# State-space angles in turns, later input tables, and other places for ada slabs, their sums and the last Toeplitz issues

## The chip, the cores and the metric

The kernel runs on 1 core of one Trainium2 chip. The metric is the device time of one execution in microseconds (us). Before the change the median of three runs is 2386.61 us (2385.92 to 2390.32).

The engines: PE is TensorE (matrix products; it also loads its weights, PEld), DVE is VectorE, ACT is ScalarE, POOL is GpSimd. SP issues most DMAs; ACT issues the others out of its own instruction queue. Each engine works its queue in order and meets the others at semaphores.

## The reference, cut to what matters

Two transformer-like blocks follow each other on 512 tokens of width 1024. The change lies in block one:

```python
z = rms_norm(x, g) @ w_in            # q k v f gf u gs qm gm gl
y_fox = forgetting_attention(q, k, v, log_f) * silu(gf)
y_s5  = gelu(s5_ssm(u, ...))         # 48 groups, 64 complex states each
y_s5  = y_s5 * sigmoid(y_s5 @ w_glu + b_glu) * silu(gs)
mk, mv = split(rms_norm(mem, g) @ w_mem_kv)
y_mem = memory_attention(qm, mk, mv) * silu(gm)
x = x + merge(y_fox, y_s5, y_mem) @ w_out
# block two needs   ada = silu(c) @ w_ada + b_ada   (two layers, 6144 columns each)
```

The state-space layer uses powers of `a = exp(lam * step)`: magnitudes, and cosines and sines of `k * Im(lam) * step` for k = 0 to 8, and of multiples of the eighth power's angle for 64 chunks of 8 tokens.

## The kernel before, in words

Weights come as slabs of 256 columns (1 MB for 1024 rows) through a ring of three slots, loaded by SP in the order of `plan_slabs` (L239). A slab's load waits until the slab three places earlier has been used up. Most slabs are then split by POOL, half by half, into a rounded high part (L234) and a rest (L236), and PE multiplies high by high, low by high and high by low (L589 in streams, L461 in tile stages). The slabs of w_glu and w_mem_kv are not split.

*ada.* Its 48 slabs are no PE work: ACT scales the slab (`ada_scale`), DVE sums it over its rows of tiles (`ada_add`, L376, 3.7 us), PE adds over partitions in a product of one column (`ada_sum`, L389) and DVE adds the bias (`ada_take`, L399). Only two sums may be under way: `ada_add` of slab n waits for `ada_sum` of n-2, and `ada_sum` of n for `ada_take` of n-1. `plan_slabs` puts an ada slab behind another slab. `tiles_stage` (L403) has ACT and DVE work on it at the tile of that slab less `ada_lead`, and has PE and DVE do sum and take three tiles later; what falls past the last tile is handed to the next stage.

*The state-space stage* (`s5_stages`, L1198) runs while PE works through a stream of 37 tiles (u, gs, q, k, f, v; 24 products each). The stream is cut at written positions: `turn_at`, `pad_at`, `out_at` say after how many products PE turns to the state space. There are six parts of 8 groups. For each part: DVE makes the drive table Bk (`drive_table`), an angle table (`angle_table`), and the output table W (`out_table`); PE turns Bk (L1441), makes the Toeplitz blocks from W (L1450), the drive (L1462), and the output y (L1475, L1476). ACT copies the Toeplitz blocks into `pad` and issues eight DMAs to lay them into TT (L1517). ACT also empties the stream's two PSUM banks, at written positions of its own queue (`stream.take`). A tile's product can't begin before the tile two earlier is taken.

*The angles.* `reduce_angle` (L1183) takes an angle in radians, finds the whole turns by adding and subtracting 1.5 * 2^23, subtracts them in three parts of 2 pi, and clamps: six DVE instructions, each waiting for the one before. It is called for the 48 step angles, for their nine multiples (432 columns, `tE`), and once a part (512 columns). ACT then takes Sin of the angle and of its half. For `tE` the half angle is one more DVE instruction (L1610). *The input tables* B1, B2 are made in two goes: part 0 alone (128 columns), and, behind the first drive and angle table, the other 40 groups (640 columns), ahead of the first W (L1686 to L1689).

*Behind the stream* come the six glu tiles (three w_glu slabs), in which ada 0 and ada 1 are worked on; then gf and qm, in whose stage the memory rows are normalised and turned; the forgetting attention; the memory keys and values (eight tiles, three ada slabs); gm with memory attention; then merge. `spread_forget` is a turn of SP bound to the slab behind glu_z2: it writes the summed gates to memory, waits for them, and reads them back spread out, 1.5 MB.

Of the kernel before, what the change touches and what calls it, by code (L numbers as in the profile page):

```python
# [10 lines left out]
ALU = mybir.AluOpType  # L11
ACT = mybir.ActivationFunctionType
# [20 lines left out]
PARTS = G5 // G6  # L33
# [10 lines left out]
TWO_PI = 2.0 * math.pi  # L44
PI_1 = 6.28125
PI_2 = float(np.float32(TWO_PI - PI_1))
PI_3 = float(TWO_PI - PI_1 - float(np.float32(TWO_PI - PI_1)))
PI_TOP = 3.1415925
LN2_1 = 0.693359375
LN2_2 = math.log(2.0) - LN2_1  # L50
ROUND = 1.5 * 2.0 ** 23
# [187 lines left out]
def plan_slabs(K, T):  # L239
# [60 lines left out]
    for i in range(3):  # L300
        add(f"glu_z{i}", T["w_glu"][0], (0, 768), 0, 768, False, part=i)
        if i < 2:
            ada(0)
# [99 lines left out]
def tiles_stage(K, tiles, banks, act=None, dve=None, act_on=None, after=None, entry=None, arriving=None, tensor_entry=None, act_lead=4,  # L403
                also=None, ada_bank=7, late=None, entry_at=None, waits=None, ada_lead=2):

# [26 lines left out]
    if ada and dve is None:  # L432
        raise ValueError("ada's slabs belong to stages in which VectorE takes the tiles")
    rest = [s for n in range(N - 3, N) for s in ada.get(n, [])]
    if late is not None:
# [10 lines left out]
    with K.stage(entry, arriving[2] if arriving else tensor_entry) as block:  # L446

        @block.tensor
        def _(pe):
# [25 lines left out]
            for n, t in enumerate(tiles):  # L475
                if n < first:
                    continue
                if entry_at is not None and n == entry_at[0]:
                    for sem, value in entry_at[1].values():
                        pe.wait_ge(sem, value)  # L480
                if n >= bufs:

                    pe.wait_ge(taken.sem, t0 + n - bufs + 1)
                if n in after:
                    pe.wait_ge(taken.sem, t0 + after[n] + 1)
                for j in range(len(t)):
                    if waits is not None and (n, j) in waits:
                        pe.wait_ge(*waits[(n, j)])
                    ins = product(n, j)
                ins.then_inc(made.sem, 1)  # L490
                for s in ada.get(n - 3, []):
                    ada_sum(K, pe, s, ada_bank)
# [28 lines left out]
        if dve is not None:  # L521
            @block.vector
            def _(e):
                for n in range(N):
# [5 lines left out]

                    for s in ada.get(n - 3, []):
                        ada_take(K, e, s, ada_bank)
# [649 lines left out]

def reduce_angle(K, e, x, t, done=None):  # L1183

# [4 lines left out]
    for part in (PI_1, PI_2, PI_3):  # L1189
        step(v.scalar_tensor_tensor(x, t, -part, x, ALU.mult, ALU.add))  # L1190
    x = v.tensor_scalar(x, x, -PI_TOP, PI_TOP, ALU.max, ALU.min)
    if done is None:
        step(x)
    else:
        x.then_inc(done.sem, 1)


def s5_stages(K, T, arriving):  # L1198
# [214 lines left out]
    with K.stage(before, arriving[2]) as block:  # L1413
# [67 lines left out]
        def _(e):  # L1481
            e.dma_start(K.scratch_x.rearrange("(t p) n -> p t n", p=P), K.xT[:, :, :]).then_inc(xa.sem, 16)
            stream.take(e, 144)
            e.wait_ge(ready.sem, 3)
            nc.scalar.activation(tB[:, :, :], tE[:, :, :], ACT.Sin).then_inc(acted.sem, 1)
            nc.scalar.activation(tC[:, :, :], tA[:, :, :], ACT.Sin).then_inc(acted.sem, 1)
            stream.take(e, START - 24)
# [9 lines left out]
            def make_sines(n):  # L1497
                e.wait_ge(angles.sem, n + 1)
                nc.scalar.activation(sinj[n % 2], cosj[n % 2][:, :, :], ACT.Sin).then_inc(sines.sem, 1)
                nc.scalar.activation(half[:, :, :], cosj[n % 2][:, :, :], ACT.Sin, scale=0.5).then_inc(sines.sem, 1)  # L1500
                e.wait_ge(sines.sem, 2 * n + 2)
# [4 lines left out]
            def lay_toeplitz(n):  # L1506
# [9 lines left out]
                for r in range(CH):  # L1516
                    e.dma_start(TT5[r * H5:(r + 1) * H5, :, :], pad[:, :, r * H5:r * H5 + P]).then_inc(laid.sem, 16)  # L1517

            def swapped(src, signal):
# [53 lines left out]
        def _(e):  # L1573
# [20 lines left out]
            step(v.tensor_tensor(angle8[:, :], lam[:, 1, :], lam[:, 2, :], ALU.mult))  # L1594
            reduce_angle(K, e, angle8[:, :], one(tA))
            kk = K.counts[:, 0:CH + 1].unsqueeze(2).broadcast_to([P, CH + 1, G5])
# [10 lines left out]
            step(v.tensor_tensor(tE[:, :, :], angle8[:, :].unsqueeze(1).broadcast_to([P, CH + 1, G5]), kk, ALU.mult))  # L1607
            reduce_angle(K, e, tE[:, :, :], tA[:, :, :])
            step(v.tensor_copy(angle8[:, :], tE[:, CH, :]))
            v.tensor_scalar(tA[:, :, :], tE[:, :, :], 0.5, None, ALU.mult).then_inc(ready.sem, 1)  # L1610
            e.wait_ge(acted.sem, 2)
# [52 lines left out]
            def angle_table(n):  # L1664
                x = cosj[n % 2][:, :, :]
                step(v.tensor_tensor(x, angle8[:, part(n)].unsqueeze(2).broadcast_to(shape2),
                                     K.counts[:, 0:NC5].unsqueeze(1).broadcast_to(shape2), ALU.mult))
                reduce_angle(K, e, x, tmp[:, :, :], angles)

# [14 lines left out]
            drive_table(0)  # L1684
            angle_table(0)
            input_table(slice(G6, G5)).then_inc(ready.sem, 1)  # L1686
            e.wait_ge(ready.sem, 4)
            v.memset(pad[:, :, 0:112], 0.0).then_inc(K.sig("pad_cleared").sem, 1)
            out_table(0)  # L1689
            for n in range(PARTS):  # L1690
# [4 lines left out]
                if n + 1 < PARTS:  # L1695
                    angle_table(n + 1)
                e.wait_ge(drive_swapped.sem, n + 1)
                e.wait_ge(cosines.sem, n + 1)
# [372 lines left out]
def mem_stages(K, T):  # L2071
# [39 lines left out]
    last = []  # L2111
    tiles_stage(K, tiles, 1, dve=dve, also=also, ada_bank=6, late=last)
    tanh.total += 6
# [865 lines left out]
```

## Time and profile before

| what | value |
|---|---|
| median of three runs | 2386.61 us |
| the profiled execution's own time | 2388.54 us |
| its span | 2386.8 us |
| PE busy | 2284.7 us, 96% |
| DVE busy | 1514.0 us, 63% |
| ACT busy | 619.7 us, 26% |
| POOL busy | 1278.5 us, 54% |
| mean granted TensorE clock | 0.981 of full |

Busy is the time in which an engine had an instruction in work. Idle time of an engine counts only where it holds up the chain that ends last. The granted clock is a share of TensorE's full 2.4 GHz; its other level, 1.2 GHz, is 0.5. In rows, "[3.39 <-DVE Bk L1657]" means that the engine was idle for 3.39 us before this instruction and that the instruction at L1657, on DVE, ended it.

### The profile page before, as it was taken

What the parts mean: (1) busy time and instruction counts of PE and PEld (TensorE: products, weight loads), DVE (VectorE), ACT (ScalarE), POOL (GpSimd) and SP (SyncE); (2) the same over time, 40 slices, a digit from 0 to 9 for tenths busy, and PEclk for the clock granted to TensorE, in tenths of its full rate; (3) what the DMA queues carried; (4) which work ended last, traced back from release to release, by engine and by line L of the source; (5) the groups of instructions that cost most, each with busy time, mean ns of one, the idle gap of its engine ahead of it and who ended that gap; (6) DMA issues with size and microseconds to landing.
All of it is one profiled execution on the core that took longest, in us unless ns stands there. A gap on an engine that the chain in (4) does not pass through costs nothing.

```text
span 2386.8 us, 29267 instructions
## 1 busy us (share of the span) xinstructions
PE 2284.7 (96%) x11773; PEld 1849.9 (78%) x11773; DVE 1514.0 (63%) x1802; ACT 619.7 (26%) x1262; POOL 1278.5 (54%) x736
## 2 busy tenths in 40 slices
PE   8898888989999999999999999999999999999998
PEld 6677756778888778777778888878877777888886
DVE  7998255564555695554789775658555477965331
ACT  3143244422221301344223332301124421300000
POOL 5453141077666566423656756666642355586662
PEclk9899999999999999999999999999999999999999
DMA  6354651234455332211344555623221132433230
GB/s 196 107 137 128 210 193 63 82 100 142 141 159 182 100 120 92 84 32 27 120 141 153 178 176 177 212 88 124 93 97 32 28 119 88 130 118 106 89 106 36
DMA packets 266578, 280.76 MB, mean 118 GB/s; under 512 B 29948, under 2 KB 238016, under 8 KB 266444
## 3 DMA queue, kind: packets, MB, share of 16 engines
q1 hardware_dynamic: 241932, 243.24, 32.5%
q10 hardware_dynamic: 24512, 35.66, 4.7%
q8 instruction: 94, 1.54, 0.3%
q14 instruction: 40, 0.33, 0.0%
HBM read 257.87 MB, written 17.85 MB: 116 GB/s over the span
## 4 chain that ended last, share of the span: by engine, by line
PE 60%; DVE 4%; ACT 0%; issue 0%; DMA 0%; POOL 0%; DVEq 0%; ACTq 0%
PE ps L461 35%; PE ps L589 7%; PE ps L2400 3%; PE ps L2401 3%; PE ps L2402 3%; PE ps L905 1%; PE ps L948 1%; PE ps L924 1%; PE ps L1094 1%; PE ps L1101 1%; PE ps L1077 1%; PE ps L2504 1%; DVE probs_b L1140 1%; PE ps L697 1%; DVE xT L798 0%; PE ps L389 0%
## 5 line engine op out<-in xcount | busy, mean ns | idle before, releaser
L234 POOL TENSOR_SCALAR ring_high<-ring 128x1024 fp32r<-128x1024 f32 (+1 forms) x342 | 398.6, 1165 | 988.2 <-PE ps L589 313.9
L236 POOL TENSOR_TENSOR ring_low<-ring,ring_high 128x1024 fp32r<-128x1024 f32 (+1 forms) x342 | 838.3, 2451 | 28.5
L461 PE MATMUL ps<-hT_high,ring_high 128*128 128x512 f32 x704 | 277.2, 394 | 0.0
L461 PE MATMUL ps<-hT_high,ring_low 128*128 128x512 f32 x704 | 274.1, 389 | 0.0
L461 PE MATMUL ps<-hT_low,ring_high 128*128 128x512 f32 x704 | 274.1, 389 | 0.0
L589 PE MATMUL ps<-hT_high,ring_high 128*128 128x512 f32 x568 | 237.0, 417 | 10.2 <-POOL ring_low L236 5.1
L589 PE MATMUL ps<-hT_high,ring_low 128*128 128x512 f32 x568 | 227.5, 401 | 0.0
L589 PE MATMUL ps<-hT_low,ring_high 128*128 128x512 f32 x568 | 227.3, 400 | 0.0
L376 DVE TENSOR_REDUCE ada_acc<-ring 128x256 f32<-128x2048 f32 x48 | 187.4, 3905 | 31.3 <-ACT ring L363 31.3
L461 PE MATMUL ps<-hidden_high,ring_high 128*128 128x512 f32 x512 | 200.1, 391 | 0.0
L461 PE MATMUL ps<-hidden_high,ring_low 128*128 128x512 f32 x512 | 199.3, 389 | 0.0
L461 PE MATMUL ps<-hidden_low,ring_high 128*128 128x512 f32 x512 | 199.2, 389 | 0.0
L2770 DVE SCALAR_TENSOR_TENSOR xT<-ps,ada,xT 128x512 f32<-128x512 f32 x64 | 48.0, 751 | 214.5 <-PE ps L461 214.5
L363 ACT ACTIVATE ring<-ring,c_act 128x256 f32<-128x256 f32 x384 | 158.3, 497 | 82.8 <-DMA ring<-in_w_ada_dram 80.6
L2400 PE MATMUL ps<-ring_high,hT_high 128*128 128x512 f32 x384 | 151.0, 393 | 5.1 <-DVE work L2447 4.2
L461 PEld LDWEIGHTS ps<-hT_high,ring_low 128*128 128x128 f32 x704 | 132.2, 188 | 27.6
L461 PEld LDWEIGHTS ps<-hT_high,ring_high 128*128 128x128 f32 x704 | 132.3, 188 | 27.2 <-DVE hT_low L783 0.2
L461 PEld LDWEIGHTS ps<-hT_low,ring_high 128*128 128x128 f32 x704 | 132.3, 188 | 26.5
L2401 PE MATMUL ps<-ring_high,hT_low 128*128 128x512 f32 x384 | 150.1, 391 | 0.0
L2402 PE MATMUL ps<-ring_low,hT_high 128*128 128x512 f32 x384 | 149.9, 390 | 0.0
L589 PEld LDWEIGHTS ps<-hT_high,ring_high 128*128 128x128 f32 x568 | 108.1, 190 | 46.7 <-issue 15.8
L2810 ACT ACTIVATE relu<-ps 128x512 f32<-128x512 f32 x64 | 38.2, 598 | 353.2 <-PE ps L461 348.1
(409 smaller groups left out, 4319.5 us busy)
## 6 DMA issues: line engine op xcount, KB each, us to landing
ring<-in_w_in_dram SPq DMA_DIRECT2D x75, 1024.0 KB, 5.2
ring<-in_w_ff_dram SPq DMA_DIRECT2D x64, 1024.0 KB, 5.3
ring<-in_w_ada_dram SPq DMA_DIRECT2D x48, 1024.0 KB, 5.4
ring<-in_w_out_dram SPq DMA_DIRECT2D x12, 1024.0 KB, 5.2
scratch_x<-xT ACTq DMA_DIRECT2D x3, 2048.0 KB, 8.3
ring<-in_w_mem_kv_dram SPq DMA_DIRECT2D x4, 1024.0 KB, 5.3
ring<-in_w_branch_a_dram SPq DMA_DIRECT2D x16, 256.0 KB, 4.0
xT<-scratch_x ACTq DMA_DIRECT2D x2, 2048.0 KB, 10.0
```

The costliest lines, as they stand in the source:

```text
L234: nc.gpsimd.tensor_scalar(hi, raw, 1.0, 1.0, ALU.mult, ALU.mult).then_inc(hi_done.sem, 1)
L236: nc.gpsimd.tensor_tensor(lo, raw, hi.bitcast(F32), ALU.subtract).then_inc(lo_done.sem, 1)
L363: ins = K.nc.scalar.activation(w[:, k, :], w[:, k, :], ACT.Copy, scale=K.c_act[:, k:k + 1])
L376: K.nc.vector.tensor_reduce(K.ada_acc[:, n % 2, :], K.slot(slab).rearrange("p k n -> p n k"), AX_X, ALU.add).then_inc(K.sig("ada_scaled"). ...
L461: return nc.tensor.matmul(out[0:rows, bank, cols[0]:cols[1]], lhsT, rhs, start=start, stop=stop)
L589: ins = K.nc.tensor.matmul(out, lhsT, rhs, start=start, stop=stop)
L697: nc.tensor.matmul(ps[:, third, 0:3 * P], K.ident, K.const[:, 0:3 * P], start=True, stop=True)
L2400: nc.tensor.matmul(out, xh, hi[:, y, :], start=k == 0, stop=False)
L2401: nc.tensor.matmul(out, xl, hi[:, y, :], start=False, stop=False)
L2402: ins = nc.tensor.matmul(out, xh, lo[:, y, :], start=False, stop=k == KD - 1)
L2770: return v.scalar_tensor_tensor(K.xT[:, m, :], ps[:, 0, :], gate[:, m:m + 1], K.xT[:, m, :], ALU.mult, ALU.add)
L2810: return nc.scalar.activation(rel[:, place[n][3] % 4, :], ps[:, 0, :], ACT.Relu)
```

## The change

1. Angles are kept in turns. `reduce_angle` is split: `turns_of` (for the 48 step angles; six instructions, the clamp replaced by a multiplication with 1/(2 pi)) and `to_whole_turns` (add 1.5 * 2^23, then one instruction that subtracts in two steps; two instructions, it leaves whole turns less the angle). ACT's scale of Sin takes the sign and 2 pi. The clamp is gone; the half angle of `tE` too, for ACT reads `tE` twice.
2. The input tables of parts 1 to 5 are made behind the first W table, and the clearing of `pad` ahead of it.
3. DVE waits for its own angle table by a semaphore before it uses X and the sines.
4. In the last part ACT takes one tile of the stream after the third and one after the sixth Toeplitz DMA.
5. The second ada slab stands behind glu_z2 and no longer between glu_z1 and glu_z2; SP's turn `spread_forget` thereby comes ahead of it.
6. In the memory stage the ada sums and takes come five tiles after their slab, not three; the last falls to the next stage.

```diff
-        if i < 2:
+        if i != 1:
             ada(0)
...
-    rest = [s for n in range(N - 3, N) for s in ada.get(n, [])]
+    rest = [s for n in range(N - ada_lag, N) for s in ada.get(n, [])]
...
-def reduce_angle(K, e, x, t, done=None):
+def turns_of(K, e, x, t):
     v = K.nc.vector
     step = lambda ins: K.link(e, "dve_step", ins)
     step(v.tensor_scalar(t, x, 1.0 / TWO_PI, ROUND, ALU.mult, ALU.add))
     step(v.tensor_scalar(t, t, ROUND, None, ALU.subtract))
     for part in (PI_1, PI_2, PI_3):
         step(v.scalar_tensor_tensor(x, t, -part, x, ALU.mult, ALU.add))
-    x = v.tensor_scalar(x, x, -PI_TOP, PI_TOP, ALU.max, ALU.min)
...
+    step(v.tensor_scalar(x, x, 1.0 / TWO_PI, None, ALU.mult))
+
+def to_whole_turns(K, e, x, t):
+    v = K.nc.vector
+    K.link(e, "dve_step", v.tensor_scalar(t, x, ROUND, None, ALU.add))
+    return v.scalar_tensor_tensor(x, t, ROUND, x, ALU.subtract, ALU.subtract)
...
-            nc.scalar.activation(tB[:, :, :], tE[:, :, :], ACT.Sin).then_inc(acted.sem, 1)
-            nc.scalar.activation(tC[:, :, :], tA[:, :, :], ACT.Sin).then_inc(acted.sem, 1)
+            nc.scalar.activation(tB[:, :, :], tE[:, :, :], ACT.Sin, scale=-TURN).then_inc(acted.sem, 1)
+            nc.scalar.activation(tC[:, :, :], tE[:, :, :], ACT.Sin, scale=0.5 * TURN).then_inc(acted.sem, 1)
...
                 for r in range(CH):
                     e.dma_start(TT5[r * H5:(r + 1) * H5, :, :], pad[:, :, r * H5:r * H5 + P]).then_inc(laid.sem, 16)
+                    if n == PARTS - 1 and r % 3 == 2:
+                        stream.take(e, out_at[n - 1] + 24 * (r // 3 + 1))
...
-            reduce_angle(K, e, tE[:, :, :], tA[:, :, :])
+            to_whole_turns(K, e, tE[:, :, :], tA[:, :, :]).then_inc(ready.sem, 1)
+            e.wait_ge(ready.sem, 3)
             step(v.tensor_copy(angle8[:, :], tE[:, CH, :]))
-            v.tensor_scalar(tA[:, :, :], tE[:, :, :], 0.5, None, ALU.mult).then_inc(ready.sem, 1)
...
             drive_table(0)
             angle_table(0)
+            v.memset(pad[:, :, 0:112], 0.0).then_inc(K.sig("pad_cleared").sem, 1)
+            out_table(0)
             input_table(slice(G6, G5)).then_inc(ready.sem, 1)
             e.wait_ge(ready.sem, 4)
-            v.memset(pad[:, :, 0:112], 0.0).then_inc(K.sig("pad_cleared").sem, 1)
-            out_table(0)
...
+                e.wait_ge(angles.sem, min(n + 2, PARTS))
                 e.wait_ge(drive_swapped.sem, n + 1)
...
-    tiles_stage(K, tiles, 1, dve=dve, also=also, ada_bank=6, late=last)
+    tiles_stage(K, tiles, 1, dve=dve, also=also, ada_bank=6, late=last, ada_lag=5)
```

`angle_table` and the sines of each part change in the same way as those of `tE`.

## Rows read from the trace of the kernel before

**Rows 1.** The page's fourth part: shares of the chain that ended last, by engine.
```profile
PE 60%; DVE 4%; ACT 0%; issue 0%; DMA 0%; POOL 0%; DVEq 0%; ACTq 0%
```
**Rows 2.** Whom PE waited for, 10 to 520 us: total us, times, longest.
```profile
PE ps L1450 <- DVE W L1657: 11.3, 3, 6.0
...
PE ps L589 <- ACT staged L1321: 4.9, 1, 4.9
```
**Rows 3.** PE in order of time, state-space stage: start, us, instruction, count, idle before.
```profile
90.84 1.97 PE L1441 MATMUL ps<-const,Bk 128*128 128x128 f32 x8 [3.39 <-DVE Bk L1657]
...
108.87 3.59 PE L1450 MATMUL ps<-W,B 128*16 128x128 f32 x16 [6.01 <-DVE W L1657]
...
128.93 1.92 PE L1450 MATMUL ps<-W,B 128*16 128x128 f32 x16
...
152.68 1.92 PE L1450 MATMUL ps<-W,B 128*16 128x128 f32 x16 [0.34 <-DVE W L1657]
...
181.00 3.60 PE L1450 MATMUL ps<-W,B 128*16 128x128 f32 x16 [4.92 <-DVE W L1657]
```
**Rows 4.** One stretch: length; busy of PE, PEld, DVE, ACT, POOL; PEclk; DMA share, GB/s.
```profile
90.00:100.00 10.00, 9.16 (x33) 7.66 (x34) 9.76 (x12) 3.94 (x6) 2.99 (x1) 0.67 0.06 18
```
**Rows 5.** DVE in order of time, from the rounding of tE to the sines.
```profile
61.00 2.46 DVE L1188 TENSOR_SCALAR tA<-tA 128x432 f32<-128x432 f32 x1
63.49 1.90 DVE L1190 SCALAR_TENSOR_TENSOR tE<-tA,tE 128x432 f32<-128x432 f32 x3
...
66.57 2.26 DVE L1609 COPY angle<-tE 128x48 f32<-128x48 f32 x1
68.86 0.39 DVE L1610 TENSOR_SCALAR tA<-tE 128x432 f32<-128x432 f32 x1
70.33 1.40 DVE L1613 TENSOR_TENSOR tC<-tC 128x432 f32<-128x432 f32 x1 [1.08 <-ACT tC L1486]
```
**Rows 6.** POOL in order of time, beside the rounding of tE.
```profile
60.81 2.40 POOL L236 TENSOR_TENSOR ring_low<-ring,ring_high 128x1024 fp32r<-128x1024 f32 x1
```
**Rows 7.** DVE by line and shape, 110 to 260 us: count, busy us, mean ns.
```profile
L1190 DVE SCALAR_TENSOR_TENSOR cosj<-rotated,cosj 128x512 f32<-128x512 f32 x15 | 10.4, 692 | 0.5
...
L1188 DVE TENSOR_SCALAR rotated<-rotated 128x512 f32<-128x512 f32 x5 | 2.1, 427 | 0.2
```
**Rows 8.** DVE in order of time: first and last of six instructions of the later input tables.
```profile
97.02 0.82 DVE L1638 TENSOR_TENSOR X<-B,f_im 128x640 f32<-128x640 f32 x1
...
100.94 1.67 DVE L1643 TENSOR_TENSOR B<-B,X 128x640 f32<-128x640 f32 x1
```
**Rows 9.** All engines in order of time, last part of the state space.
```profile
254.30 0.63 ACT L1520 ACTIVATE swapped<-scanned 64x512 f32<-64x512 f32 x1 [5.26 <-issue]
...
256.67 2.72 DVE L1714 TENSOR_TENSOR state<-cosj,rotated 128x504 f32<-128x504 f32 x1
...
260.94 0.33 PE L1475 MATMUL ps<-U,TT 128*128 128x64 f32 x2
```
**Rows 10.** SP in order of time, glu stage.
```profile
299.28 0.37 SPq L209 DMA_DIRECT2D ring<-in_w_ada_dram  x1
308.23 0.37 SPq L209 DMA_DIRECT2D ring<-in_w_glu_dram  x1
```
**Rows 11.** PE in order of time, glu stage.
```profile
312.82 8.21 PE L461 MATMUL ps<-yP,ring 128*128 128x512 f32 x12 [3.27 <-DMA ring<-in_w_glu_dram]
...
321.24 5.40 PE L461 MATMUL ps<-yP,ring 128*128 128x512 f32 x12
327.64 0.50 PE L589 MATMUL ps<-hT_high,ring_high 128*128 128x512 f32 x1 [1.01 <-POOL ring_low L236]
```
**Rows 12.** PE in order of time, memory keys and values.
```profile
479.28 0.98 PE L389 MATMUL ps<-const,ada_acc 128*128 128x1 f32 x4 [2.63 <-DVE ada L399]
480.12 9.92 PE L461 MATMUL ps<-ring,memT 128*128 128x256 f32 x32
...
495.52 0.50 PE L589 MATMUL ps<-hT_high,ring_high 128*128 128x512 f32 x1 [1.58 <-POOL ring_low L236]
```

More of the change, by code:

```diff
@@ L47 @@
 PI_3 = float(TWO_PI - PI_1 - float(np.float32(TWO_PI - PI_1)))
-PI_TOP = 3.1415925
+TURN = 2.0 * 3.1415925
 LN2_1 = 0.693359375
@@ L403, in tiles_stage @@
 def tiles_stage(K, tiles, banks, act=None, dve=None, act_on=None, after=None, entry=None, arriving=None, tensor_entry=None, act_lead=4,
-                also=None, ada_bank=7, late=None, entry_at=None, waits=None, ada_lead=2):
+                also=None, ada_bank=7, late=None, entry_at=None, waits=None, ada_lead=2, ada_lag=3):
     nc, ps = K.nc, K.ps
@@ L490, in _ @@
                 ins.then_inc(made.sem, 1)
-                for s in ada.get(n - 3, []):
+                for s in ada.get(n - ada_lag, []):
                     ada_sum(K, pe, s, ada_bank)
@@ L529, in _ @@
                     dve(e, n, view(n)).then_inc(taken.sem, 1)
-                    for s in ada.get(n - 3, []):
+                    for s in ada.get(n - ada_lag, []):
                         ada_take(K, e, s, ada_bank)
@@ L1190, in reduce_angle @@
         step(v.scalar_tensor_tensor(x, t, -part, x, ALU.mult, ALU.add))
-    x = v.tensor_scalar(x, x, -PI_TOP, PI_TOP, ALU.max, ALU.min)
[L1192 to L1195, printed above, removed]
+    step(v.tensor_scalar(x, x, 1.0 / TWO_PI, None, ALU.mult))
[3 more added lines that the diff above has]
+    return v.scalar_tensor_tensor(x, t, ROUND, x, ALU.subtract, ALU.subtract)
 def s5_stages(K, T, arriving):
@@ L1498, in make_sines @@
                 e.wait_ge(angles.sem, n + 1)
-                nc.scalar.activation(sinj[n % 2], cosj[n % 2][:, :, :], ACT.Sin).then_inc(sines.sem, 1)
-                nc.scalar.activation(half[:, :, :], cosj[n % 2][:, :, :], ACT.Sin, scale=0.5).then_inc(sines.sem, 1)
+                nc.scalar.activation(sinj[n % 2], cosj[n % 2][:, :, :], ACT.Sin, scale=TURN).then_inc(sines.sem, 1)
+                nc.scalar.activation(half[:, :, :], cosj[n % 2][:, :, :], ACT.Sin, scale=0.5 * TURN
+                                     ).then_inc(sines.sem, 1)
                 e.wait_ge(sines.sem, 2 * n + 2)
@@ L1594, in _ @@
             step(v.tensor_tensor(angle8[:, :], lam[:, 1, :], lam[:, 2, :], ALU.mult))
-            reduce_angle(K, e, angle8[:, :], one(tA))
+            turns_of(K, e, angle8[:, :], one(tA))
             kk = K.counts[:, 0:CH + 1].unsqueeze(2).broadcast_to([P, CH + 1, G5])
@@ L1667, in angle_table @@
                                      K.counts[:, 0:NC5].unsqueeze(1).broadcast_to(shape2), ALU.mult))
-                reduce_angle(K, e, x, tmp[:, :, :], angles)
+                to_whole_turns(K, e, x, tmp[:, :, :]).then_inc(angles.sem, 1)
             def out_table(n):
```

## Prediction

> **What bounds the kernel now.** First the chain that ended last, by engine: 60% of it is TensorE and 4% VectorE [rows 1], so a microsecond counts where PE stands idle or runs slowly. Then the waits of PE in block one: the largest is 11.3 us in three waits for the output table W, ended by VectorE; next a single 4.9 us for ACT to empty a bank [rows 2]. In order of time PE waits 3.39 us for the drive table Bk at 90.84, then 6.01, 0.34 and 4.92 us for W [rows 3]. The reader is to see that in this stage DVE, not PE, sets the pace: the fourth W ends it at 181.00 although two parts before stood almost without a wait. A wait costs more than itself. Behind 6.01 and 4.92 us of idleness the same 16 products take 3.59 and 3.60 us, behind 0 and 0.34 us they take 1.92 [rows 3]; from 90 to 100 us, behind 3.39 us, the granted clock is 0.67 on average, a mixture of 1.2 and 2.4 GHz [rows 4].
>
> **Edit 1, angles in turns.** The step angles keep six instructions: no change. For tE, old: from the start of the second rounding step at 61.00 to DVE's next dependent work at 70.33 are 9.33 us [rows 5]. New: at 61.00 stands the one three-operand instruction, 1.90 / 3 = 0.63 with its gap; then ACT's two sines, which end 1.08 us after the last instruction; the copy of 48 columns lies beside them [rows 5]. So 9.33 - 0.63 - 1.08 = 7.6 us less. But two of those rows hold more than work: 2.46 us for what takes 0.39 at L1610, and 2.26 for a copy of 48 columns [rows 5]. POOL's subtraction runs from 60.81 to 63.21 just then [rows 6]. If such delay is met by whatever instruction comes next, only the plain work goes: the second rounding step, the clamp and the half angle at 0.39 each, two three-operand instructions at 0.63, and 0.2 for the copy: 2.6, with gaps 2.7 us. The head gives 2.7 to 7.6.
>
> The Trainium skill's page "SBUF — State Buffer" (section "Who interferes with whom") says that a DVE instruction with two SBUF inputs, or in a two-port mode, and a GpSimd instruction exclude each other for the whole instruction. This trace agrees as to the first rows, 2.46 against 0.39 us; by it the low end of the head, 2.7, would hold, since a lock not met by a removed instruction is met by the next.
>
> Each part's angle table, plain: old three one-input instructions of 0.427 and three of 0.692, with six gaps of about 0.035: 3.57; new one of each and two gaps: 1.19 [rows 7]. 2.4 us a part. Four tables (parts 0 to 3) lie before the W that ended the 4.92 us wait: 9.5. DVE's chain to 181.00 shortens by 12.2 to 17.1; I take the middle, 14.5, so this W comes at 166.5.
>
> **Edit 2, later input tables.** Six instructions, 97.02 to 102.61, 5.6 us [rows 8], leave the way of W 0 and enter the way of Bk 1. To the fourth W it is neutral; it only moves the idle time. Bk 0 comes 2.7 to 7.6 us earlier against 3.39 wanted; W 0 comes 5.6 + 2.4 us more than that earlier, 10.7 or more. PE itself, without waits: it would be at the first turn at 87.45, and needs 1.0 for it (half of 1.97), 36 products at 0.227 us (from start to start at full rate) = 8.2, 1.9 for the Toeplitz products, about 2.0 drive, 54 products 12.3, 1.0 turn: second Toeplitz products at 113.8. One part lasts 152.68 - 0.34 - 128.93 = 23.4 us [rows 3], so the fourth W is wanted at 113.8 + 46.8 = 160.6. DVE has it at 166.5. PE thus still waits some 6 us, spread over the first three W tables in pieces below the present ones; an unmoved W 0 would have gathered them early. Gain to there 181.0 - 166.5 = 14.5. With short pieces the Toeplitz products run at 1.92 and no longer 3.60, and the 12 behind them at full rate (3.4 against 2.9): 2.1 more. **16.6 us**, with bounds 12.2 (all DVE bound, the clock still falls) and 22.5 (PE bound: 181.0 - 160.6 + 2.1). In the fifth and sixth part ACT, not DVE, holds PE; that stays.
>
> **Edit 3, the wait for its own angle table** takes the place of the link that the clamp had; what is queued behind is DVE's own rotation. 0; at most six semaphore turns of 0.04.
>
> **Edit 4, last Toeplitz issues.** The 4.9 us wait [rows 2] shrinks to about 0.5, since a tile is taken after three issues. But y of this part also wants the state, which wants ACT's swapped copy at 254.30 and then DVE's 0.95 + 2.72 us, ended at 259.39; PE starts y at 260.94 [rows 9]. ACT now issues two takes (0.38 us each) and a DMA ahead of that copy: some 1.2 us later. So y can start 0 to 1.9 us earlier, and PE stands idle some 5 us right before it; today the half rate falls on the 24 products ahead of y, then it would fall on y itself, up to 2 us. **0**, bounds -2 (loss) and +1.9 (gain).
>
> **Edit 5, second ada slab behind glu_z2.** SP loads what takes the place of today's ada slab at 299.28, and glu_z2 at 308.23 [rows 10]. With the new order glu_z2 goes at 299.28, 8.9 us earlier, and PE's 3.27 us wait is gone. So is the half rate behind it: 12 instructions in 8.21 us against 5.40 [rows 11], 2.8. The first gf slab may also go earlier, since spread_forget, SP's turn in front of it, no longer waits behind glu_z2's late load; its split ended PE's 1.01 us [rows 11]. It then shares its way with the ada slab: 0.0 of this counted. Against it: DVE's sum of the ada slab (3.7 us) now stands behind the sixth glu tile, in front of the casts and the reciprocal that the memory rows' turning on PE needs. In the profile DVE idles there for 1.2 and 5.8 us, which hides most of it; I let what is left over cancel against a 0.5 us wait of PE for the last glu tile, which goes. **6.1 us**, bounds 3.3 and 7.6.
>
> **Edit 6, sums five tiles later.** PE's 2.63 us wait for DVE's take goes, and 32 instructions that took 9.92 us (two tiles; the next two took 3.7 each at full rate) lose 2.5; the 1.58 us for POOL behind it [rows 12] may go too, since the fourth tile ends sooner. But ada_add of the third slab must wait for ada_sum of the first, which now follows the sixth tile; behind it on DVE stand two gates (1.4 us each), two copies and the take that PE's second sum waits for. From PE's sixth tile, ended at 480.7 (472.93 for the fifth's start, two tiles at 3.7, 0.4 for the sum): 3.7 + 1.8 + 1.8 + 0.2 = 488.2, against PE at 484.8 behind the seventh tile: a new wait of 3.4 us, perhaps with a slow last tile. gm then starts at 492 to 494.8, not 495.52; the late sum adds 0.5. **1.8 us**, bounds -0.5 and +3.
>
> **The sum.** 16.6 + 0 + 0 + 6.1 + 1.8 = 24.5 us. All later work moves with PE. Against the profiled execution (2388.54; span 2386.8) this gives 2364.0; the median of the runs is 1.9 lower, so 2386.6 - 24.5 = 2362.1.
>
> **Rivals.**
> The first: delay by POOL is passed on wherever an instruction goes, the new sums stall PE as above, and y loses 2 us at the low clock. For it: the two rows of 2.46 and 2.26. Against: three-operand instructions beside POOL at 63.49 took 0.63. The gain is 12.2 + 2.1 + 6.1 - 0.5 - 2 = 17.9; 2368.7.
> The second: PE, not DVE, binds from the first part on; then the fourth W is there at 160.6. For it: 7.6 in the head is what the rows' stamps give. Against: W 1 has the input tables before it. 22.5 + 6.1 + 1.8 = 30.4; 2356.2.
> The third: the glu and memory edits only exchange waits (the ada slab and gf share the DMA engines, POOL starts late, the memory rows are turned late). 16.6 alone: 2370.0.
> The fourth, slower: delay of DVE by POOL grows. PE without waits makes POOL's splits come denser, and DVE meets each with a two-input instruction. One met costs about 2.1 us (2.46 - 0.39), and POOL splits 13 halves between 70 and 181 us. Today's fourth W already holds most of it. To turn 24.5 gained into 5 lost, the 13 halves must cost 29.5 / 13 = 2.3 us each more than now, over double. It decides from there: 2392 or more. Against: a POOL pair is 3.5 us long and cannot hold DVE longer.
>
> **Chances.** Forecast 0.55 (its own range 2358 to 2366.5), the first 0.17, the second 0.13, the third 0.10, the fourth 0.02; 0.03 that nothing measurable comes out. About 0.2%, 5 us, is what can be told from no change. Faster 0.95, same 0.03, slower 0.02. The range 2354 to 2371 takes in the first three rivals.
>
> **What would show it.** Bk 0: no wait of PE at L1441. L1450: each wait under 3 us, the fourth Toeplitz products near 166, 1.92 us long. Angle tables in three instructions. The last y at its distance from the drive, with idleness now in front of L1475. glu: no DMA wait in front of the fifth tile, 5.4 us for it. Memory: the wait moves from the first L389 to the second, 3 us. Wrong it would be if L1450 still shows waits over 4 us, if y starts later than before relative to its drive by over 2 us, or if PE waits for the memory rows' turning over 2 us.

## The result and the profile after

The changed kernel takes 2371.44 us (median of 4 runs, 2368.03 to 2376.52), the kernel before 2388.27 on the same chip: ratio 0.9932, 95% interval 0.991 to 0.9953. Two repeats gave 0.9943 (0.9931 to 0.9955) and 0.9939 (0.9926 to 0.9951). By the medians the gain is 13 to 17 us. 24.5 were forecast, and 2371.44 lies just outside the range of 2354 to 2371. The profiled execution took 2371.07 us (span 2369.2, before 2386.8).

The waits of PE, 10 to 505 us, in the changed kernel (total us, times, longest), against [rows 2]:

```profile
PE ps L589 <- POOL ring_low L236: 7.7, 3, 3.2
PE ps L1480 <- DVE state L1723: 5.3, 1, 5.3
PE ps L1455 <- DVE W L1665: 4.4, 3, 2.6
PE ps L1446 <- DVE Bk L1665: 4.1, 1, 4.1
```

The 11.3 us for W are 4.4, and the 4.9 us for ACT's staged rows are gone. Two waits have taken their places: 4.1 us for a drive table, 5.3 us for the state in front of y. (Of the 7.7 us for POOL, 1.46 stand in the glu stage, below; none of it stands between the head and the end of the state space.) PE in order of time, state-space stage, against [rows 3]:

```profile
88.85 1.03 PE L1446 MATMUL ps<-const,Bk 128*128 128x128 f32 x8
98.84 1.92 PE L1455 MATMUL ps<-W,B 128*16 128x128 f32 x16 [0.76 <-DVE W L1665]
...
112.65 1.46 PE L1446 MATMUL ps<-const,Bk 128*128 128x128 f32 x8 [4.14 <-DVE Bk L1665]
124.81 1.92 PE L1455 MATMUL ps<-W,B 128*16 128x128 f32 x16 [2.62 <-DVE W L1665]
...
148.18 1.92 PE L1455 MATMUL ps<-W,B 128*16 128x128 f32 x16
...
172.63 1.92 PE L1455 MATMUL ps<-W,B 128*16 128x128 f32 x16 [1.05 <-DVE W L1665]
```

The first drive table comes without a wait. The first W is 12.6 us sooner, measured from PE's first product of the stage's head (swap with C: 41.45 us before, 43.99 after; this start lay between 41.5 and 45.2 in every kernel of this study, so stages are compared from it). Half of that is lost again at 112.65 and 124.81. The fourth W's distance is 181.00 - 41.45 = 139.55 us before and 172.63 - 43.99 = 128.64 after: 10.9 us, not 14.5. DVE at the place of [rows 5]:

```profile
62.39 1.12 DVE L1199 TENSOR_SCALAR tA<-tE 128x432 f32<-128x432 f32 x1
63.54 2.68 DVE L1200 SCALAR_TENSOR_TENSOR tE<-tA,tE 128x432 f32<-128x432 f32 x1
66.25 0.19 DVE L1618 COPY angle<-tE 128x48 f32<-128x48 f32 x1
67.37 0.61 DVE L1621 TENSOR_TENSOR tC<-tC 128x432 f32<-128x432 f32 x1 [0.93 <-ACT tC L1491]
68.01 1.12 DVE L1622 TENSOR_SCALAR tC<-tC 128x432 f32<-128x432 f32 x1
69.16 2.69 DVE L1623 TENSOR_TENSOR pow_re<-tC,tD 128x432 f32<-128x432 f32 x1
```

The two instructions of 2.46 and 2.26 us are gone. In their stead the one kept three-operand instruction takes 2.68 (0.63 per instruction before), and the next product with two SBUF inputs 2.69. POOL beside them:

```profile
61.90 1.36 POOL L234 TENSOR_SCALAR ring_high<-ring 128x1024 fp32r<-128x1024 f32 x1 [1.80 <-PE ps L589]
63.35 2.40 POOL L236 TENSOR_TENSOR ring_low<-ring,ring_high 128x1024 fp32r<-128x1024 f32 x1
```

So the delays have two sizes: 0.7 us (1.12 for what takes 0.39) beside POOL's short instruction, and 2.1 us (2.68 for 0.61) beside its long one. The end of the state space, against [rows 9] (the last row counts two of 32 instructions; they run without a gap to 255.85):

```profile
246.31 2.10 DVE L1719 TENSOR_TENSOR rotated<-swapped,xT 128x512 f32<-128x512 f32 x1 [4.12 <-ACT swapped L1529]
249.19 0.69 PE L1480 MATMUL ps<-U,TT 128*128 128x64 f32 x2 [5.25 <-DVE state L1723]
```

```profile
249.00:256.00 7.00, 6.81 (x32) 0.50 0.01 2
```

The second fence is the stretch in which y is made (length, PE busy, granted clock, DMA share, GB/s): 0.50 of full speed, 1.2 GHz, behind 5.25 us of idleness. y takes 6.66 us; before it took 3.46. PE in the glu stage, against [rows 11], and in the memory stage, against [rows 12]:

```profile
304.47 5.40 PE L461 MATMUL ps<-yP,ring 128*128 128x512 f32 x12
311.32 0.50 PE L589 MATMUL ps<-hT_high,ring_high 128*128 128x512 f32 x1 [1.46 <-POOL ring_low L236]
```

```profile
454.84 7.17 PE L461 MATMUL ps<-ring,memT 128*128 128x256 f32 x32 [1.49 <-DMA ring<-in_w_mem_kv_dram]
464.48 5.38 PE L461 MATMUL ps<-ring,memT 128*128 128x256 f32 x16 [2.13 <-DMA ring<-in_w_mem_kv_dram]
470.41 0.58 PE L389 MATMUL ps<-const,ada_acc 128*128 128x1 f32 x4 [0.55 <-DVE ada L399]
```

The DMA wait and its half rate in glu are gone, as forecast. In the memory stage the wait for the sum is short in this execution, but PE waits for two slabs.

### The profile page after: what moved, and what is told of

Same layout as the page of the kernel before. It is cut to its first block, busy times and chain, and to the rows that moved or that the text cites. A ratio compares the mean times of both kernels' runs of the same rounds, so it can differ in the third digit from the quotient of the medians.

```text
span 2369.2 us, 29239 instructions
## 1 busy us (share of the span) xinstructions
PE 2276.7 (96%) x11773; PEld 1848.7 (78%) x11773; DVE 1496.8 (63%) x1773; ACT 620.0 (26%) x1262; POOL 1285.8 (54%) x736
## 4 chain that ended last, share of the span: by engine, by line
PE 61%; DVE 4%; ACT 0%; issue 0%; DMA 0%; POOL 0%; DVEq 0%; ACTq 0%
PE ps L461 35%; PE ps L589 7%; PE ps L2409 3%; PE ps L2410 3%; PE ps L2411 3%; PE ps L905 1%; PE ps L948 1%; PE ps L924 1%; PE ps L1094 1%; PE ps L1101 1%; PE ps L1077 1%; PE ps L697 1%; PE ps L2513 1%; DVE probs_b L1140 1%; DVE xT L798 0%; PE ps L389 0%
## 5 line engine op out<-in xcount | busy, mean ns | idle before, releaser
L589 PEld LDWEIGHTS ps<-hT_high,ring_high 128*128 128x128 f32 x568 | 107.8, 190 | 44.8 <-issue 16.3
```

The source lines that it names most:

```text
L589: ins = K.nc.tensor.matmul(out, lhsT, rhs, start=start, stop=stop)
```

## The experiments

Theory 1: DVE sets the pace up to the fourth W, and what POOL holds it up is a fixed toll. An instruction that is removed takes its own work along, not the delay it met. Theory 2: the gain went into the order of the tables (the 4.1 us wait). Theory 3: what is missing is scatter between executions.

**The changed kernel again, and its halves.** `again` and `third` are the changed kernel; `before_again` is the kernel before.

> The changed kernel a second time. Theory A: 2.5 us of its profile (the stream's first products late) are scatter of the first input transfers, and another 2.7 us behind 790 us are the clock in the norm between the blocks; a second profile then has the swap of the C table (PE, L1437) anywhere from 41 to 44.5 us, and the time lies in 2366 to 2372. Rival B: both come from the change, so the C swap stands at 44 again, the rotary stage stands 17.5 us earlier than before the change, and the time is 2371 again.

> The kernel before, unchanged, profiled a second time. Theory A (which VectorE instruction meets which POOL instruction shifts by some tenths from run to run, and the state-space stage with it): up to the fourth Toeplitz products the distance from the C swap is 139.6 to 142.5 us (the kernel with only the ada edits, whose state-space code is the same, had 142.2), VectorE's time over its shortest 40 to 47 us in 18 pairs of POOL instructions. Theory B (the profile of before is typical): every distance within 0.5 us of the first profile.

`again`: 2376.1 us (5 runs), 4 to 5 us above both expectations. The start moved to 44.98, outside Theory A's 41 to 44.5; but kernels with the head of before start late too (43.34 in `ada_only`), so the late start is not the change's. The fourth W came 127.67 us behind it. `before_again`: 2390.41 (10 runs), ratio 1.0008; 140.71 to the fourth W, as its Theory A had it, and 52.11 us from the first glu product to the memory rows' turning, where the first profile had 55.20. So a single profile carries 1 us of scatter up to the fourth W and 3 in a later stage. Theory 3 does not cover 9 us in the times, but forbids reading a term from one pair of traces.

`state_space_only` has edits 1 to 4 (`if i < 2: ada(0)` and three tiles again); `ada_only` is the kernel before with edits 5 and 6.

> Angles in turns, later input tables, the Toeplitz takes; ada slabs and sums at their old places. Theory A: this half gains 13 us up to the last drive (counted from the C swap on PE), gives back 2 at the last y, and gets 1.6 in the glu tiles: 12 to 13 us in all. Rival: the DVE chain gains as forecast and the ada edits give nothing: 17 us or more here.

> The kernel before, with the second ada slab behind glu_z2 and the sums five tiles later in the memory stage. Theory A: 10 us faster than before (6.8 in the glu stage, 3.4 in the memory stage). Rival: the glu stage's gain exists only because the state space ended earlier and the transfers beside it were other ones: 4 us or less.

2380.78 us, ratio 0.9958 (0.9942 to 0.9974), about 10 us gained where 16.6 were forecast; and 2384.91, 0.998 (0.9972 to 0.9989), 4.8 us where 7.9 were. Both forecasts were too high, and so were the expectations of 12 to 13 and of 10 us. In `ada_only` the glu stage did give what Theory A said (46.9 us against 52 to 55), but the time shows about half of it. The two halves add up to 15 us, the gain of the whole.

**Only the angles.** The kernel before with edits 1 and 3.

```
-            reduce_angle(K, e, tE[:, :, :], tA[:, :, :])
+            to_whole_turns(K, e, tE[:, :, :], tA[:, :, :]).then_inc(ready.sem, 1)
...
-                reduce_angle(K, e, x, tmp[:, :, :], angles)
+                to_whole_turns(K, e, x, tmp[:, :, :]).then_inc(angles.sem, 1)
```

> The kernel before with the angles in turns alone (edit 1, with the wait of edit 3). Theory A (only the plain work of the removed instructions is gained, and the order of the tables is worth some more by itself): the fourth Toeplitz products 5 to 8 us sooner behind the C swap than in before, the Bk 0 wait gone, the first W 4 us sooner; 2380-2386, a gain of 4 to 9 us. Theory B (the order of the tables is neutral): 10 to 12 us sooner, as in the whole change, and the same time as with edits 1 to 4, 2378-2381.

2377.29 us, 0.9956 (0.9941 to 0.9971); the fourth W at 130.25. The time is that of all four edits together, as Theory B of the expectation had it; the fourth W lies between the two. As far as the times can tell, this edit carries the whole gain of the state space.

**Edit 2 undone.**

```
+            input_table(slice(G6, G5)).then_inc(ready.sem, 1)
+            e.wait_ge(ready.sem, 4)
             v.memset(pad[:, :, 0:112], 0.0)...
             out_table(0)
-            input_table(slice(G6, G5)).then_inc(ready.sem, 1)
-            e.wait_ge(ready.sem, 4)
```

> The changed kernel with the later input tables back in front of the first W table. Theory A (the move only redistributes VectorE's work): the first Toeplitz products come 5 to 6 us later, PE's 4.1 us wait for the second drive table is gone, the fourth Toeplitz products stay within 1.5 us of 128.6 behind the C swap, and the time is within 3 us of the changed kernel (2371-2377). Theory B (the wait for the second drive table is where the missing gain went): the fourth Toeplitz products come 3 to 4 us sooner, the time is 2367-2371. Theory C (the move itself pays): 3 us or more slower, 2378 or more.

2376.33 us, 0.9939 (0.9924 to 0.9954): the time of the changed kernel. The 4.1 us wait is gone, the waits for W are 10.3 us again (9.2 in one). The fourth W came at 133.83, worse than expected, where `angles_only` with the same order had 130.25. The order is neutral in time, as its Theory A had it, and Theory 2 falls: with its wait gone nothing was gained.

**POOL's second instruction made short.** The test of Theory 1, in the kernel before and in the changed one. Both versions leave out the subtraction: the low halves hold a scaled copy and not the rest of the split. Their results are wrong, and they serve for their times alone.

```
+        if K.first["gs"] <= i < K.first["glu_z0"]:
+            nc.gpsimd.tensor_scalar(lo, raw, 2.0 ** -13, 1.0, ALU.mult, ALU.mult).then_inc(lo_done.sem, 1)
+            continue
         nc.gpsimd.tensor_tensor(lo, raw, hi.bitcast(F32), ALU.subtract).then_inc(lo_done.sem, 1)
```

> The kernel before, in which POOL's second split instruction (the low half, two inputs, 2.46 us on a full slab half) of the slabs from gs to v is a one-input instruction as short as the first (1.17 us); those low halves hold wrong numbers. Theory A (in the state-space stage VectorE is held by POOL, and this sets the pace): from the C swap to the fourth Toeplitz products VectorE was busy 133.1 us, of which 41.5 are over the shortest time seen for the same instruction; the 41.5 fall by half or more, the fourth Toeplitz products come 15 to 20 us sooner behind the C swap (from 139.6 to 120 to 125, where PE itself binds), and the time falls by 12 to 20 us, to 2370-2377. Theory B (the long instructions have another cause, or the pace is set elsewhere): the 41.5 stay within 5, the time within 4 us of 2389.

> The same edit in the changed kernel, with the same wrong low halves. Theory A: the 45.4 us of VectorE over its shortest times fall by half or more; the fourth Toeplitz products come at 117 to 122 us behind the C swap instead of 128.6, and the time falls by 6 to 12 us to 2360-2368. The gap between the two kernels with the short instruction is smaller than between the whole ones (2 to 10 us for the whole change, the ada edits among it, against 17), since PE then binds in both. Theory B: nothing moves by more than 4 us, and the gap of the two stays 13 to 18 us.

2369.85 us, 0.9914 (0.9897 to 0.993), and 2364.29, 0.9886 (0.9867 to 0.9906): Theory A in both (21 us in the first, a little over its 12 to 20). The gap between the two kernels is 5.6 us, where the whole ones lie 13 to 17 apart. The split instructions of POOL from 44 to 173 us of the changed kernel, by line (count, busy, mean ns), and from 41 to 165 of the one with the short instruction:

```profile
L236 POOL TENSOR_TENSOR ring_low<-ring,ring_high 128x1024 fp32r<-128x1024 f32 x18 | 52.8, 2932 | 1.5
L234 POOL TENSOR_SCALAR ring_high<-ring 128x1024 fp32r<-128x1024 f32 x18 | 27.6, 1532 | 50.3 <-PE ps L589 39.3 <-DMA ring<-in_w_in_dram 10.9
```

```profile
L237 POOL TENSOR_SCALAR ring_low<-ring 128x1024 fp32r<-128x1024 f32 x18 | 27.5, 1527 | 1.5
```

What that does to DVE, 84 to 220 us, first in the changed kernel, then with the short instruction (same columns):

```profile
L1663 DVE TENSOR_TENSOR t<-pow_im,C 128x1152 f32<-128x1152 f32 x6 | 15.8, 2640 | 0.2
...
L1709 DVE TENSOR_TENSOR swapped<-ps,cosj 128x512 f32<-128x512 f32 x5 | 3.5, 691 | 0.2
```

```profile
L1666 DVE TENSOR_TENSOR t<-pow_im,C 128x1152 f32<-128x1152 f32 x6 | 10.3, 1722 | 0.2
```

The same table product takes 2.64 us in the mean beside the long instruction and 1.72 beside the short one (its shortest is 1.36). The rotation that reads one operand from PSUM takes 0.69 in every row. Between the start and the last y no row of PE, in any of the four kernels, waits for POOL, so the gain comes through DVE. In the changed kernel with the short instruction PE then has no wait for a table at all (in the other one of 0.79 us):

```profile
99.01 1.92 PE L1458 MATMUL ps<-W,B 128*16 128x128 f32 x16
...
116.77 1.92 PE L1458 MATMUL ps<-W,B 128*16 128x128 f32 x16
...
140.11 1.92 PE L1458 MATMUL ps<-W,B 128*16 128x128 f32 x16
...
163.44 1.81 PE L1458 MATMUL ps<-W,B 128*16 128x128 f32 x15
```

Summed over all rows of DVE between the start and the fourth W, with "over" for each duration less the shortest of the same instruction and shape in any of the profiles:

```
kernel             distance   instructions   busy    shortest   over
before              139.6         150        133.1     87.1     46.0
before_again        140.7         149        133.9     86.6     47.3
ada_only            142.2         147        132.9     86.1     46.8
angles_only         130.2         128        123.9     75.3     48.6
changed             128.6         126        121.9     74.8     47.1
third               127.7         128        120.0     75.2     44.8
no_tables           133.8         128        122.9     75.2     47.7
pieces              133.4         143        122.7     76.7     46.0
short_low_before    119.3         151        112.1     88.5     23.6
short_low_after     118.4         129         99.4     76.0     23.4
```

This is the main finding. Over 14 profiles of eleven kernels with the long instruction (eight profiles of them above), "over", the toll, is 44.8 to 48.6 us whether DVE issues 126 instructions or 150, while POOL splits 18 halves (17 in some profiles, by where the stretch is cut). That is 2.6 us for each half. The rows show what it is made of: in every one of the 14 profiles 13 to 16 instructions of DVE take 0.6 to 0.95 us over their shortest and 15 to 17 take 1.9 to 2.3 over; with the short form 28 and 29 take 0.6 to 0.95 over, and none 1.9. So some 30 of POOL's 36 instructions delay one of DVE's each, by about 0.3 us less than its own shortest time: 0.7 for 1.04 us, 2.1 for 2.39. The edit took 12.3 us of plain work, and none of the toll. A late pace cannot be the cause either: `short_low_before` reaches the fourth W at 119.3 with 13 us more work on DVE than `short_low_after`, so at 118 to 119 us PE itself binds (one wait of 0.79 us for a table is left in the first kernel, none in the second); the prediction had this bound at 119.1 (160.6 - 41.45).

The Trainium skill's page "SBUF — State Buffer" (section "Who interferes with whom") says that a DVE instruction with two SBUF inputs or in a two-port mode and a GpSimd instruction that reads SBUF hold each other off for whole instructions, and that DVE with at most one SBUF input, outside the two-port modes, does not contend. The trace agrees: 2.64 and 0.69 us above. Copies and roundings with one SBUF input are delayed too (last section); no row shows in which mode they run.

**The tables part by part**, meant as a better version: part 1's input table where all stood, the later ones in DVE's wait for ACT's swapped scan.

```
-            input_table(slice(G6, G5)).then_inc(ready.sem, 1)
+            input_table(part(1)).then_inc(ready.sem, 1)
...
                 step(v.tensor_tensor(co, Gs[:, :, :], co, ALU.mult))
+                if n + 2 < PARTS:
+                    step(input_table(part(n + 2)))
```

> The changed kernel with the later input tables made part by part: part 1's (a fifth of the 5.6 us, with fixed costs about 1.2) where the whole stood, parts 2 to 5 each in VectorE's wait for ScalarE's swapped copy of the scan. Theory A (VectorE's chain sets the pace up to the fourth W): PE's wait for the second drive table falls from 4.1 us to under 0.5, the fourth Toeplitz products come 3 to 5 us sooner than at 128.6 behind the C swap, the time is 3 to 5 us below the changed kernel, 2367-2372. Theory B (what VectorE saves POOL's turn takes back, or the last parts bind otherwise): the fourth Toeplitz products within 1.5 us, the time 2371-2377.

2380.14 us, 0.9957 (0.9944 to 0.997): 4 to 9 us slower than the changed kernel by the medians, which neither theory had. The profiled execution took 2386.89 us, the slowest of the six (the others 2377.78 to 2380.58), so its waits may be larger than in the others. DVE in its order of time, with POOL's instruction beside it:

```profile
148.44 0.29 DVE L1647 TENSOR_TENSOR input_scratch<-B,f_im 128x128 f32<-128x128 f32 x1
...
148.97 1.01 DVE L1649 TENSOR_TENSOR B<-B,f_re 128x128 f32<-128x128 f32 x1
...
150.22 2.37 DVE L1651 TENSOR_TENSOR B<-B,input_scratch 128x128 f32<-128x128 f32 x1
...
165.56 0.69 DVE L1709 TENSOR_TENSOR rotated<-swapped,sinj 128x512 f32<-128x512 f32 x1 [3.02 <-ACT swapped L1530]
```

```profile
149.93 2.51 POOL L236 TENSOR_TENSOR ring_low<-ring,ring_high 128x1024 fp32r<-128x1024 f32 x1
```

```profile
155.00 0.43 PE L1481 MATMUL ps<-U,TT 128*128 128x64 f32 x2 [1.94 <-DVE state L1726]
...
160.62 3.62 PE L1468 MATMUL ps<-U,BkT 128*128 128x64 f32 x16
```

An instruction of 0.28 us lasts 2.37: the toll does not ask for its size. The six small ones put 4.4 us in front of the state, PE waits 1.94 us for it, runs most of y and the drive at half rate (3.62 against 1.95 us), and DVE idles 3.02 us for the drive that this made late. The place looked free (1.14 us of idleness in the changed kernel's second part), but was on the way of the state. That this makes up the whole loss is likely, but was not tried.

**Edit 4 undone, and edit 6 undone.**

```
-                    if n == PARTS - 1 and r % 3 == 2:
-                        stream.take(e, out_at[n - 1] + 24 * (r // 3 + 1))
```

> The changed kernel without ACT's two takes between the last part's Toeplitz DMAs. Theory A: PE waits 4.9 us for the bank instead of 5.3 for the state; the half rate falls on 24 products ahead of y, y starts about 1 us later against its drive and runs at full rate; the whole is within 1 us of the changed kernel, rather faster. Rival: the takes are worth the 3 us of the removed wait, so this one is 2 to 3 us slower.

```
-    tiles_stage(K, tiles, 1, dve=dve, also=also, ada_bank=6, late=last, ada_lag=5)
+    tiles_stage(K, tiles, 1, dve=dve, also=also, ada_bank=6, late=last)
```

> The changed kernel with the sums of the ada slabs in the memory stage three tiles behind again (edit 6 undone). Theory A (the sum's wait only moves from the first sum to the second, 2.5 us at either place): the time within 1.5 us of the changed kernel's. Theory B (the predicted 1.8 us): slower by 1.5 to 3 us.

2371.29 us (0.9933, 0.9919 to 0.9946) and 2371.82 (0.9928, 0.9912 to 0.9945): neither is slower than the changed kernel, as Theory A had it in both. Both were then undone at once, beside the changed kernel on one chip.

> The changed kernel with edits 4 and 6 both undone (edits 1, 2, 3 and 5 stay). Theory A (the two edits cost what their stages show: about 2.1 us from the last drive products to the first glu product, and 0 to 1.5 us in the memory stage, each by half rate behind a wait): that stretch is 42.2 us and not 44.3, y takes 3.5 us and not 6.7, and the time is 2 to 4 us below the changed kernel of the same call. Theory B (what they cost is taken back later, or is less than the scatter of the state-space stage): within 1.5 us of it.

> The changed kernel once more, to be set against one_two_five on the same chip. Theory A: 2371-2377, 2 to 4 us above one_two_five; 44.3 us from the last drive products to the first glu product; the fourth Toeplitz products 127 to 131 us behind the C swap. Theory B: the same time as one_two_five.

2369.39 us (5 runs), 0.9918 (0.9905 to 0.9931), against 2374.76 (6 runs), 0.9939 (0.9926 to 0.9951): 5.4 us faster in the medians (2 to 4 were expected), though the intervals overlap. It has the lowest median of all versions that leave nothing out. ACT in `third`, the last part:

```profile
240.35 0.38 ACT L1326 ACTIVATE staged<-ps 128x256 f32<-128x256 f32 x1 [2.00 <-issue]
...
245.06 0.63 ACT L1528 ACTIVATE swapped<-scanned 64x512 f32<-64x512 f32 x1 [2.36 <-issue]
```

and ACT and PE in `one_two_five`:

```profile
243.79 0.63 ACT L1526 ACTIVATE swapped<-scanned 64x512 f32<-64x512 f32 x1 [5.25 <-issue]
...
245.52 0.58 PE L589 MATMUL ps<-ring_high,hT_high 128*128 128x256 f32 x1 [4.89 <-ACT staged L1326]
...
250.81 0.52 PE L1480 MATMUL ps<-U,TT 128*128 128x64 f32 x2
```

The takes put ACT's copy 1.5 us later behind the last drive products (245.06 - 234.13 = 10.9 against 243.79 - 234.32 = 9.5; 1.2 were forecast), and move PE's 4.9 us of idleness from before 24 products to before y. y starts 1.4 us sooner behind the drive (15.06, 16.49) and takes 6.66 us instead of 3.79.

**Edit 5 undone.**

```
-        if i != 1:
+        if i < 2:
             ada(0)
```

> The changed kernel with the second ada slab back ahead of glu_z2 (edit 5 undone). Theory A (edit 5 is worth what its stage shows, 8 us between the first glu product and the turning of the memory rows): that stretch takes 55 us and not 47, and the time rises by 4 to 8 us, to 2376-2382. Theory B (it is given back in the memory stage or by the clock): within 2 us of the changed kernel's.

2376.07 us, 0.9951 (0.9936 to 0.9965), the least that Theory A allowed; the stretch takes 51.8 us, and not 55. PE shows the old wait and its half rate:

```profile
304.14 6.80 PE L461 MATMUL ps<-yP,ring 128*128 128x512 f32 x12 [3.26 <-DMA ring<-in_w_glu_dram]
```

**All profiles by stage**, since one pair misleads. Without the two short-low kernels and `pieces`; us from PE's rows:

```
stretch                                       edit absent            edit present           gain
start to fourth W            (edits 1, 2)     139.6 140.7 142.2      127.7 to 133.8 (10)    11.2
start to last drive products (edits 1, 2)     203.4 204.1 207.2      190.0 to 198.2 (10)    11.8
last drive to first glu      (edit 4)         41.6 to 42.7 (6)       44.1 to 44.6 (7)       -2.2
first glu to memory rows     (edit 5)         51.8 to 55.3 (5)       46.8 to 47.2 (8)        6.8
memory K and V               (edit 6)         41.6 to 44.9 (6)       41.2 to 46.7 (7)       -0.7
```

Gains are differences of the means; profiles in brackets. Of the ten with edits 1 and 2, two have edit 1 alone (`angles_only`, `no_tables`). Memory K and V runs from their first product to the first of memory attention. The gains add up to 15.7 us (with the stretch to the last drive, which holds the one to the fourth W), against 13 to 17 in the times.

## Why the prediction was wrong

The direction and most places held; the sum was 8 to 11 us too high. By stages, 24.5 - 15.7 = 8.8 us are missing: 4.8 in the state space up to the last drive, 2.2 at the last y, 2.5 in the memory stage, with 0.7 more than forecast in glu. The mechanism of the first rival (17.9 us), held at 0.17, was the right one. Step by step:

- **Edit 1, "I take the middle, 14.5".** This step failed. The bounds were 12.2 (plain work) and 17.1 (with the delays of the two rows). The measured plain work is 12.3 us [rows 5, 7], the toll that went with it none (46.0 to 47.3 us before, 44.8 to 48.6 after). The low bound was the answer, and about 1 us more of toll and 0.2 of idleness leave 10.9. The trace of before already had what was needed. POOL's count of splits does not change with DVE's. And the one reason given against the first rival, "three-operand instructions beside POOL at 63.49 took 0.63", was misread: POOL's subtraction had ended at 63.21 [rows 6], and its next instruction began at 64.87, so the first two of the three had nothing beside them. The clamp at 65.42, which did stand beside it, took 1.12 us for 0.39.

```profile
64.87 1.43 POOL L234 TENSOR_SCALAR ring_high<-ring 128x1024 fp32r<-128x1024 f32 x1 [1.66 <-PE ps L589]
```

- **Edit 1, the clock's 2.1 us.** The fourth Toeplitz products did run at full rate (1.92 against 3.60), and in the first pair of profiles the stretch behind them gave 2.3 us more (13.2 to the last drive). In the means it gave 0.6: 11.2 us to their start, 11.8 to the last drive, where 16.6 were summed. From the fourth W to the last drive the profiles with the edit differ by 4 us among themselves; what takes the rest of this term is not shown. DVE's idleness up to the fourth W, 6.3 to 10.9 us in the table above, stays open too.
- **Edit 2, neutral.** Right in the time. "Each wait under 3 us" held for W in the three profiles of the changed kernel (up to 2.6); `no_lag`, with the same code in this stage, had 3.4 and 4.7. The wait at 112.65 was not forecast, though the prediction named the six instructions (5.6 us) that enter the way of this table. The fourth Toeplitz products were looked for near 166 and came at 172.63; 2.5 us of this is the later start.
- **Edit 3, 0.** Nothing in any profile speaks against it; it was never tried alone.
- **Edit 4, 0 within -2 and +1.9.** Measured -2.2, just beyond the lower bound. The mechanism was the one named: idleness right before y, and half rate on y. y takes 3.2 us more (32 small products in 6.66 instead of 3.46) and starts only 1.1 to 1.4 us sooner behind the drive.
- **Edit 5, 6.1.** Measured 6.8 in its stage; in the times the edit is worth 2 to 4.5 us (0.9951 against 0.9932 to 0.9943), and 5 together with edit 6 (`ada_only`). Where the rest goes is not shown. The DMA wait, the half rate and the row 5.40 came as forecast; PE's wait for POOL stayed (1.46 against 1.01).
- **Edit 6, 1.8 within -0.5 and +3.** Measured -0.7, inside the scatter of 5 us of this stage. In five of the seven profiles with the edit the sum's wait only moved to the second sum (2.5 to 2.9 us), as forecast at 3.4. Not forecast were two DMA waits, 1.2 to 1.6 and 1.9 to 2.3 us, where the profiles without the edit have one of 1.0 to 2.4. The 64 products of the last four tiles take 16.2 us with the edit, and 14.6 (`no_lag`) to 17.3 (before) without. PE's wait of 1.5 us for POOL in front of gm goes, as thought possible. That the later sums release the slabs' places later is the likely cause, but was not tried.
- **The rivals.** The second (PE binds from the first part on) is refuted by the waits; its bound itself is real, for the short-low kernels reach 118.4 to 119.3. The third (glu only exchanges waits) is refuted by 6.8 us. The fourth (the toll doubles) is refuted: it does not change.

## What to carry to other kernels

Where DVE and POOL both work from SBUF and DVE is rarely idle, count POOL's instructions in the stretch and charge DVE nearly the shortest length of each (0.7 us for 1.04, 2.1 for 2.39; some 30 of 36 were met here). Removing a DVE instruction saves its shortest duration only, however long its row is. What moves such a stage is POOL's work (21 us in the kernel before from one shorter instruction form, though no run here has a short form that keeps the result right). Before PE's idleness is moved, price the half rate on what will stand behind it.

## What was not expected of the hardware

- The delay of DVE by POOL goes by POOL's instruction and not by DVE's: 2.1 us beside the long one, whether 0.28 us became 2.37 or 1.36 became 3.44. It holds for instructions with one SBUF input as well, where input and output lie in SBUF (a copy of 504 columns 0.40 to 2.63 us, a rounding of 512 columns 0.43 to 2.52), and never for the rotation from PSUM (0.69 in all 96 rows).
- It is mutual: POOL's long instruction takes 2.39 us at its shortest and 2.93 in the mean of the changed kernel's state-space stage.
- The start (the swap with C) lies at 41.5 to 45.2 us over the 16 profiles, and the same kernel's differs by 1 us (43.99, 44.98 and 44.14; 41.45 and 42.27), before any edit acts.
